# The finished rows of a pair of heads are turned in bank 7 instead of bank 6, in the first block's attentions

## What is computed

```python
def hybrid_layer(x, w_in, f_bias, lam_vec, subln, w_out, g_pre, g_post, layer_idx, cos, sin):
    h = rms_norm(x, g_pre)
    p = h @ w_in
    ...
    ya = merge(diff_attention(qa, ka, heads(va, N_HEADS_DIFF, DIFF_V_DIM), lam, lambda_init, subln))
    ya = ya * jax.nn.silu(ga)
    yb = merge(stick_breaking_attention(heads(qs, ...), heads(ks, ...), heads(vs, ...)))
    yb = yb * jax.nn.silu(gs)
    ...
    yc = merge(forgetting_attention(heads(qf, ...), heads(kf, ...), heads(vf, ...), cum_log_f))
    yc = yc * jax.nn.silu(gf)
    y = jnp.concatenate([ya, yb, yc], axis=-1) @ w_out
    return x + rms_norm(y, g_post)
```

## Time and profile before

| | us |
|---|---|
| three runs, lowest, median, highest | 2048.58, 2050.96, 2052.0 |
| the profiled execution's own time | 2051.6 |
| its span, first to last instruction | 2049.8 |
| mean granted clock of PE, share of full | 0.966 |
| PE busy | 1941.4 (95%) |
| ACT busy | 886.3 (43%) |
| DVE busy | 773.1 (38%) |
| POOL busy | 661.9 (32%) |

### The profile page before, as it was taken

One profiled execution on the slowest core, in us unless ns is written; L12 is line 12 of the kernel. 1 busy time (PEld: TensorE's weight loads), 2 busy tenths in 40 slices (PEclk: granted clock), 3 DMA queues, 4 the chain that ended last, 5 costly groups with the idle time before them and its releaser, 6 DMA issues.

```text
span 2049.8 us, 25677 instructions
## 1 busy us (share of the span) xinstructions
PE 1941.4 (95%) x9552; PEld 1599.9 (78%) x9552; DVE 773.1 (38%) x1393; ACT 886.3 (43%) x1741; POOL 661.9 (32%) x278
## 2 busy tenths in 40 slices
PE   8998998998899899899889999999999989999998
PEld 6877787877777778787767788888788878888886
DVE  3434655344543555534444682111251431111102
ACT  4555564344455555444444652333453353322222
POOL 2422231321224132132123354434303424344442
PEclk9999999997899999999889999999999989999999
DMA  4221211211322112121032223222201322323222
GB/s 149 83 72 42 72 62 51 74 62 43 133 75 80 52 62 64 50 83 60 34 136 92 81 94 102 83 93 92 82 1 58 128 83 93 103 93 99 97 93 92
DMA packets 44572, 163.80 MB, mean 80 GB/s; under 512 B 6192, under 2 KB 6448, under 8 KB 43824
## 3 DMA queue, kind: packets, MB, share of 16 engines
q1 hardware_dynamic: 42640, 148.65, 21.9%
q10 hardware_dynamic: 1824, 13.63, 1.8%
HBM read 155.97 MB, written 6.29 MB: 79 GB/s over the span
## 4 chain that ended last, share of the span: by engine, by line
PE 83%; DVE 8%; ACT 5%; issue 3%; DMA 0%; POOL 0%; DVEq 0%; ACTq 0%; POOLq 0%; SPq 0%
PE bank L578 12%; PE bank L579 12%; PE bank L580 12%; PE bank L581 10%; PE bank L583 10%; PE bank L582 10%; PE bank L691 3%; PE bank L709 2%; PE bank L669 2%; PE bank L715 2%; PE bank L670 1%; ACT q_dup L904 1%; PE bank L711 1%; PE bank L667 1%; PE bank L631 1%
## 5 line engine op out<-in xcount | busy, mean ns | idle before, releaser
L561 POOL TENSOR_TENSOR w_hl<-w_raw,w_hl 128x1024 fp32r<-128x1024 f32 x274 | 661.7, 2420 | 1363.5 <-ACT w_hl L792 1362.8
L792 ACT ACTIVATE w_hl<-w_raw 128x1024 fp32r<-128x1024 f32 x274 | 287.4, 1058 | 344.8 <-DMA w_raw<-wstream 344.2
L578 PE MATMUL bank<-act_hl,w_hl 128*128 128x512 f32 x1056 | 428.2, 405 | 3.2 <-DVE act_hl L1135 2.5
L580 PE MATMUL bank<-act_hl,w_hl 128*128 128x512 f32 x1056 | 414.6, 393 | 0.0
L579 PE MATMUL bank<-act_hl,w_hl 128*128 128x512 f32 x1056 | 414.1, 392 | 0.0
L581 PE MATMUL bank<-w_hl,act_hl 128*128 128x512 f32 x672 | 265.7, 395 | 4.0 <-POOL w_hl L561 1.9
L583 PE MATMUL bank<-w_hl,act_hl 128*128 128x512 f32 x672 | 262.9, 391 | 0.0
L582 PE MATMUL bank<-w_hl,act_hl 128*128 128x512 f32 x672 | 262.7, 391 | 0.0
L578 PEld LDWEIGHTS bank<-act_hl,w_hl 128*128 128x128 f32 x1056 | 200.7, 190 | 45.6 <-DVE act_hl L1135 2.9
L580 PEld LDWEIGHTS bank<-act_hl,w_hl 128*128 128x128 f32 x1056 | 199.8, 189 | 43.7
L579 PEld LDWEIGHTS bank<-act_hl,w_hl 128*128 128x128 f32 x1056 | 200.6, 190 | 40.0 <-issue 1.9
(11 more groups left out here) (216 smaller groups left out, 2907.9 us busy)
## 6 DMA issues: line engine op xcount, KB each, us to landing
w_raw<-wstream SPq DMA_DIRECT2D x274, 512.0 KB, 3.4
x_spill<-x_res ACTq DMA_DIRECT2D x2, 2048.0 KB, 6.9
x_res<-x_spill ACTq DMA_DIRECT2D x2, 2048.0 KB, 7.9
x_res<-x SPq DMA_DIRECT2D x4, 512.0 KB, 6.3
g_post<-post_gains ACTq DMA_DIRECT2D x4, 512.0 KB, 3.8
x_res<-x ACTq DMA_DIRECT2D x1, 2048.0 KB, 7.8
out<-x_res SPq DMA_DIRECT2D x4, 512.0 KB, 2.6
probs<-w_gates ACTq DMA_DIRECT2D x1, 1024.0 KB, 9.7
```

Of the source, the lines that this page charges most:

```text
L561: nc.gpsimd.tensor_tensor(w_hl[:, slot, 1].rearrange("p c n -> p (c n)"), w_raw[:, slot, :], w_hl[:, slot, 0].rearrange("p c n -> p (c n)" ...
L578: pe.matmul(out_ap, wh, ah, start=start, stop=False)
L580: return pe.matmul(out_ap, wl, ah, start=False, stop=stop)
L792: nc.scalar.activation(w_hl[:, b % RING, 0].rearrange("p c n -> p (c n)"), w_raw[:, b % RING, :], ACT.Copy).then_inc(s_high_done, 1)
```

## The change

In plan(), the heads' turn of the first block takes bank 7 (BO) in place of bank 6 (BT). The dilated attention of the second block keeps bank 6.

```diff
             if n in HEADS_AT[kind] and part == 1:
                 p = HEADS_AT[kind].index(n)
-                take(("Y", l, kind, p), BT)
+                take(("Y", l, kind, p), BT if kind == "dil" else BO)
                 mark("y_high", (l, kind, p))
                 mark("y_low", (l, kind, p))
```

## The result

| | before | with the change |
|---|---|---|
| median of the runs, us | 2049.77 (4 runs, 2047.19 to 2052.0) | 2035.01 (4 runs, 2030.11 to 2037.35) |
| ratio, 95% interval | | 0.9926 [0.9907, 0.9945] |
| the profiled execution, us | 2051.6 | 2037.35 |
| its span, us | 2049.8 | 2035.5 |
| mean granted clock | 0.966 | 0.971 |

The change makes the kernel 0.7% faster, 14.8 us between the medians and 14.3 us between the two profiled executions. I had forecast 9 us, 2042, with a range from 2036 to 2048: the direction was right, the gain was about 1.6 times the forecast, and the time lies just outside the range.

What follows compares the result with a forecast made beforehand. PE, busy 95% of the span, was taken to bound the kernel; 12.1 us saved in sb and fox less 3.1 lost in diff gave 9.0 us, from 2050.96 to 2042.0 us, range 2036 to 2048.

Steps and rivals of the forecast that it cites:

- What bounds the kernel: PE, busy 95% of the span; before L726 it waits 12 times for DVE's L1323, 16.4 us, for the bank alone.
- The saving in sb and fox, as idle time: L726 starts earlier at sb n = 11, 13, 16 and fox n = 12, 14, 16: 6.06 us a layer, 12.1 in both.
- The losses in diff, as idle time: L726 waits for L1340: 1.56 us lost at n = 10, none at n = 13 and 16; 3.1 us in both layers.
- The sum as idle time: Whole kernel: 12.1 us gained in sb and fox less 3.1 lost in diff, 9.0 us.
- The clock: Half-clock stretches: 0 to 3.4 us lost behind diff n = 10, some perhaps gained in sb and fox; taken as cancelling.
- My own sign of being wrong: Whole kernel: the forecast is wrong if the share of half clock changes by more than two or three stretches.
- the clock comes back: Rival, chance 0.10: without the stalls in sb and fox four half-clock stretches end, 9.0 + 6.8 us, so 2035.

Runs made afterwards that it cites:

- the kernel with diff alone: Heads' turn in bank 7 in diff only, sb and fox left in bank 6, against the kernel before: 2055.6 us, ratio 1.0028.
- the one with work at sb n = 13: The change plus 22 extra transposes ahead of that heads' turn in both layers: 2033.69 us, ratio 0.9933 to the kernel before.

## Why the prediction went wrong

- **What bounds the kernel** (PE, and the waits of L726 for a bank that holds a stranger's data): right. The 12 waits for L1323 are gone.
- **The saving in sb and fox, as idle time:** right in sb, to the hundredths at n = 11 and n = 16. DVE followed as worked out: the idle time of the stage of n = 13 falls from 4.9 to 2.0 us, by the 2.9 of the wait. In the tail of fox it falls by 0.6 us in layer 0 and 1.8 in layer 1; I had 1.08 in each, so there only the sum is right.
- **The losses in diff, as idle time:** right in the main. L726 waits 1.88 and 2.87 us, the 2.64 us at L669 are used up, the values wait 0.84 us, the 2.60 at L581 become 1.66. The shift of equal instructions behind n = 10 is 1.23 us; I had 1.56, and n = 13 adds nothing to it, as forecast. The stage's idle time grows by 1.65 us all the same, since PE, faster than before, meets a new wait of 0.57 us at a later L581: that this comes out at my 1.56 is luck.
- **The sum as idle time:** 9.0 forecast, 8.7 measured.
- **The clock:** this step failed. I wrote that the new stall in diff might bring half-clock stretches and that the going stalls might take some with them, and "I take these as cancelling". They don't. Half clock went from both stages of sb n = 13 (6.8 us each; PE is busy 1.9 and 2.0 us less there) and from behind L581 in diff (3.4 us each; 1.7 and 1.5 us less, which about makes up for diff's idle time); against that, the stall at n = 10 brought none in the profile of the change. The term I set at 0 is 5.6 us in the profiled pair, by PE's busy time, all parts of the kernel together. My own sign of being wrong came with it: the half clock fell from 137.9 to 117.2 us, by six stretches net, where I had allowed two or three.
- **It is not one lucky profile:** the mean clock is 0.971 to 0.976 in all nine executions of the change and 0.964 to 0.973 in the 62 of the kernel before that ran beside the experiments.
- What should have told me was in the rows: in the earlier trace rows L691 and L726 run at half clock around the very stall that goes, and in the earlier trace rows the half clock follows the very wait that I let shrink from 2.60 to 1.6 us. I had both, the first as a hint for the rival "the clock comes back", and gave that 0.10, where it should have been a term of the sum. That rival's 2035 is what came, and partly by luck: it counted four stretches in fox and sb worth 6.8 us, while eight went from sb, diff and fox, worth 8.1 us, and the rest of the kernel took 2.5 back.

## What to carry to other kernels

A wait on the engine that sets the end can have two prices: its length, and the clock that falls with it. Look in the windows at the granted clock around each long wait. Where it is half, half of PE's busy time in that stretch may belong to the wait's price, and a change that only shortens the wait can win it. Whether it does belong to it takes a test, since the clock may have fallen ahead of the wait: put work in the place of the wait and see whether the clock holds. Split a difference between two profiles with equal instruction counts into idle time and busy time first; two rows do it. And compare stages rather than totals where a stage elsewhere changes its time from one execution to the next.

Where a bank is waited for by count, ask whose data the last user left there: turn a product into the bank whose drain is earliest in the draining engine's order, which here is another bank in sb and fox than in the first pairs of diff. And where idle stretches can't be removed, useless work in them may pay. Here it did at the last turn of diff, in fox and in the norms, and far less than expected in fox with the banks left as they were.

## What the runs showed of the hardware

- Extra PE work made the kernel faster: 72 transposes in the tails of fox, ratio 0.9862 [0.9847, 0.9877] against 0.9903 [0.9883, 0.9923]. 10 transposes in a wait of 2.6 us made their stage 0.6 us shorter (53.37 against 53.95 us, layer 1).
- A wait of 3.20 us cost 5.45 us, work of 2.40 us in its place 2.35.
- With a wait of 2.60 us (L581 in diff) the clock fell to half at its end or shortly behind it ten times of ten; with the same wait at 1.51 to 1.66 us it stayed up 18 times of 18.
- At 1.88 and 1.90 us it went both ways: behind the stall at diff n = 10 it fell in 2 of 10 places (layer 0 of the kernel with diff alone and of the one with work at sb n = 13), behind that at sb n = 11 in 3 of 8 (none in the kernel before). At sb n = 13 two waits of some 1 us each were all that stood shortly ahead of the fall in the kernel before; in the change the clock stayed up behind them. So a single profile can't settle a wait of such a length.
- In the tail of fox the same program ran 27.3 us at half clock in one execution and 23.9 in another.
- With fillers in the tails of fox and at three norms the mean clock of the kernel is 0.992; before it is 0.966.
